# Sample tokens' attention and the merge of attention groups beside head 0's projection, instead of in a stage of their own

## The reference

```
proj = rms_norm(x) @ w_in          # attention q/k/v of 3 groups | DeltaNet q/k/v | z | beta | decay | gates
# for each group g, head h:
s = q_g . k_g * HD_A**-0.5 + bias_g          # keys at distances 0, d, 2d, ..., window
m = max(s); p = exp(s - m); den = sum(p)
o_g = (p / den) @ v_g;   lse_g = m + log(den)
o_a = sum_g softmax_g(lse_g) * o_g           # the merge of the groups
# branch B: gated DeltaNet, 8 heads, chunk by chunk: conv + silu on q/k/v, recurrence, gated norm
mix = sigmoid(gate_a) * (o_a @ w_branch_a) + sigmoid(gate_b) * (o_b @ w_branch_b)
x = x + rms_norm(mix @ w_out);  x = x + rms_norm(ffn(rms_norm(x)))
```

## Time and profile before

| what | value |
|---|---|
| time, median of 3 runs (lowest, highest) | 2573.39 us (2572.24, 2573.95) |
| the profiled execution's own time | 2572.3 us |
| its span, first to last instruction | 2570.5 us |
| TensorE busy (matmul) | 2314.8 us, 90% |
| VectorE, ScalarE, GpSimd busy | 1068.8, 649.0, 30.4 us |
| mean granted TensorE clock | 0.93 |

### The profile page before, as it was taken

One profiled execution on the slowest core, in us unless ns is written; L12 is line 12 of the kernel. 1 busy time (PEld: TensorE's weight loads), 2 busy tenths in 40 slices (PEclk: granted clock), 3 DMA queues, 4 the chain that ended last, 5 costly groups with the idle time before them and its releaser, 6 DMA issues. The chain is left out here.

```text
span 2570.5 us, 35425 instructions
## 1 busy us (share of the span) xinstructions
PE 2314.8 (90%) x13936; PEld 2149.8 (84%) x13936; DVE 1068.8 (42%) x1959; ACT 649.0 (25%) x1428; POOL 30.4 (1%) x28
## 2 busy tenths in 40 slices
PE   5888988559999999999999688796999999979898
PEld 3677877459999999999999588576999999958676
DVE  4123221344776666667666533442222222231233
ACT  4122222103233332323323210442111111131221
POOL 0000000000000000000000000000000000000000
PEclk6999988559999999999999899898999999989999
DMA  4010201411121221212212153623221222050432
GB/s 149 18 64 11 81 11 50 146 29 49 46 70 35 78 58 45 76 28 78 58 45 91 45 168 111 195 84 91 74 71 60 72 67 74 25 173 24 140 110 62
DMA packets 209578, 190.33 MB, mean 74 GB/s; under 512 B 30243, under 2 KB 180804, under 8 KB 209478
## 3 DMA queue, kind: packets, MB, share of 16 engines
q1 hardware_dynamic: 196090, 144.12, 19.1%
q10 hardware_dynamic: 11120, 36.96, 3.7%
q0 software_dynamic: 2304, 8.39, 1.4%
HBM read 138.05 MB, written 51.59 MB: 74 GB/s over the span
## 5 line engine op out<-in xcount | busy, mean ns | idle before, releaser
L270 PE MATMUL bank<-xT_hi,w_lo 128*128 128x344 f32 x1152 | 394.3, 342 | 3.6 <-DVE w_lo L266 3.6
L272 PE MATMUL bank<-xT_hi,w_hi 128*128 128x344 f32 x1152 | 369.4, 321 | 0.0
L271 PE MATMUL bank<-xT_lo,w_hi 128*128 128x344 f32 x1152 | 369.2, 320 | 0.0
L270 PE MATMUL bank<-xT_hi,ffn_lo 128*128 128x344 f32 x1056 | 338.7, 321 | 11.4 <-DVE ffn_lo L266 11.4
L272 PE MATMUL bank<-xT_hi,ffn_hi 128*128 128x344 f32 x1056 | 338.2, 320 | 0.0
L271 PE MATMUL bank<-xT_lo,ffn_hi 128*128 128x344 f32 x1056 | 337.6, 320 | 0.0
L270 PEld LDWEIGHTS bank<-xT_hi,w_lo 128*128 128x128 f32 x1152 | 218.7, 190 | 3.7 <-issue 3.7
L271 PEld LDWEIGHTS bank<-xT_lo,w_hi 128*128 128x128 f32 x1152 | 218.7, 190 | 0.0
L272 PEld LDWEIGHTS bank<-xT_hi,w_hi 128*128 128x128 f32 x1152 | 217.6, 189 | 0.0
L270 PEld LDWEIGHTS bank<-xT_hi,ffn_lo 128*128 128x128 f32 x1056 | 199.5, 189 | 11.5 <-issue 11.5
L272 PEld LDWEIGHTS bank<-xT_hi,ffn_hi 128*128 128x128 f32 x1056 | 199.3, 189 | 0.0
(11 more groups left out here) (364 smaller groups left out, 4106.1 us busy)
## 6 DMA issues: line engine op xcount, KB each, us to landing
w_raw<-in_w_in SPq DMA_DIRECT2D x48, 512.0 KB, 3.9
ffn_raw<-in_w_ffn_in SPq DMA_DIRECT2D x44, 512.0 KB, 5.0
act_scr<-ffn_y ACTq DMA_DIRECT2D x22, 516.0 KB, 2.7
fo_sr<-act_scr SPq DMA_DIRECT2D x16, 704.0 KB, 6.7
fo_wr<-in_w_ffn_out SPq DMA_DIRECT2D x22, 512.0 KB, 5.4
gate_scr<-gate ACTq DMA_DIRECT2D x16, 516.0 KB, 3.3
a_kv_raw<-in_w_in SPq DMA_DIRECT2D x3, 2048.0 KB, 9.2
mix_ta<-gate_scr SPq DMA_DIRECT2D x8, 516.0 KB, 4.9
```

What stands on the lines that cost most here:

```text
L270: nc.tensor.matmul(out, stat_lo, mov_hi, start=start, stop=False)
L271: nc.tensor.matmul(out, stat_hi, mov_lo, start=False, stop=False)
L272: return nc.tensor.matmul(out, stat_hi, mov_hi, start=False, stop=stop)
```

## The change

`sample_attention_block` is gone, and the `clear_semaphores` behind it. Its work stands in `heads_block`, between the steps of head 0's projection. `pipelined` takes a `prologue` for each engine, which gets the `Filler` of head 0 and says between which steps what stands. In detail:

- The queries are no longer spread by TensorE. VectorE writes them to `q_row`, a DMA takes them to `q_scr` in DRAM, and a DMA for each group reads them back for all 128 partitions (`q_all`, 8 KB for each partition). The product with the keys reads both operands from SBUF, 2,048 columns in one instruction.
- Keys and values of the caches are loaded apart (`sa_k`, two buffers; `sa_v`), over tiles that the recurrence uses later. The constants' rows lie in `sa_v` too.
- The own keys and values take a way through DRAM (`kvs_scr`, three more small stores in `attention_block`).
- The merge: only denominators and maxima (`m_stats`, runs of 8 numbers) go to VectorE, which makes the weights; the adding up is done by GpSimd (`merge_rows`), token tile by token tile, five instructions of 256 columns and one load of `m_x` for each of 8 tiles. The result `merged` is turned at the head of `pair_block("mix")`. `os_` keeps the denominators and maxima behind the outputs for that.
- `ub` is cleared behind the prologue, after `merge_over`; TensorE, ScalarE and GpSimd wait for it (`cleared`) before the recurrence.
- GpSimd clears the norm stage's 15 semaphores inside `attention_block`; the single `clear_semaphores` behind `heads_block` has 152 to clear (before: 75 and 100).

```diff
-        def sample_attention_block():
-            with ExitStack() as s, nc.Block() as block:
...
+            def scores(v, g):
+                k = NKEY[g]
+                v.wait_ge(k_ld[g % 2], 16 * (g // 2 + 1))
+                v.wait_ge(q_ld, 16 * g + 16)
+                nc.vector.tensor_tensor(k_c[g % 2][:k], k_c[g % 2][:k], q_all[:k], ALU.mult).then_inc(vec, 1)
+                made(v, "q_used", 2 * g + 1)
+                nc.vector.reduce_sum(sc[:k, g], k_c[g % 2][:k].rearrange("p b (h d) -> p (b h) d", h=HA), AX.X
+                                     ).then_inc(vec, 1)
...
+                for t in range(NT):
+                    pool.wait_ge(x_ld[t % 2], 16 * (t // 2) + 16)
...
+                    nc.gpsimd.tensor_tensor(y, of[0], weight[0], ALU.mult)
+                    nc.gpsimd.tensor_tensor(of[1], of[1], weight[1], ALU.mult)
+                    nc.gpsimd.tensor_tensor(of[2], of[2], weight[2], ALU.mult).then_inc(row, 1)
+                    pool.wait_ge(row, 3 * t + 1)
+                    nc.gpsimd.tensor_tensor(y, y, of[1], ALU.add).then_inc(row, 1)
+                    pool.wait_ge(row, 3 * t + 2)
+                    nc.gpsimd.tensor_tensor(y, y, of[2], ALU.add).then_inc(row, 1)
+                    pool.wait_ge(row, 3 * t + 3)
+                    if t + 2 < NT:
+                        fetch(t + 2)
...
-                    constants_turn(pe)
-                    constants_over(pe)
-                    pipelined(pe, project_pe, recur_pe, lag=0)
+                    def prologue(fill):
+                        sa_turn_q(pe)
+                        constants_turn(pe)
+                        constants_over(pe)
+                        sa_bias(pe)
+                        fill.upto(SC_STEP)
+                        sa_turn_sc(pe)
+                        fill.upto(P_STEP)
+                        sa_turn_p(pe)
+                        fill.upto(PV_STEP)
+                        sa_products(pe)
+                        fill.finish()
+                        pe.wait_ge(cleared, 1)
...
+                    def prologue(fill):
+                        fill.upto(1)
+                        merge_exps(act)
+                        fill.upto(SC_STEP)
+                        sa_exps(act)
+                        fill.finish()
+                        nc.scalar.preload_act_table_set("natural_log_exp_and_others")
+                        act.wait_ge(cleared, 1)
...
-                    nc.vector.memset(ub[:], 0.0).then_inc(cleared, 1)
-                    constants_take(v)
+                    def prologue(fill):
+                        sa_q(v)
+                        constants_take(v)
+                        merge_weights(v)
+                        fill.upto(1)
+                        sa_scores(v, 0)
+                        fill.upto(76)
+                        sa_scores(v, 1)
+                        fill.upto(88)
+                        sa_scores(v, 2)
+                        fill.upto(SC_STEP - 3)
+                        sa_softmax(v)
+                        sa_probs(v)
+                        fill.upto(PV_STEP - 2)
+                        sa_take(v)
+                        fill.finish()
+                        merge_over(v)
+                        nc.vector.memset(ub[:], 0.0).then_inc(cleared, 1)
```

More of the change, by code:

```diff
@@ L502, in attention_block, with _ @@
                 oso = [sem("a_oso") for _ in range(2)]
-                KVO = (2, 5, 9)
+                KVO = (3, 6, 10)
                 done = sums(NT * [KT + 1])
                 SPLIT_Q = 4
+                @block.gpsimd
+                def _(pool):
+                    for x in used:
+                        pool.sem_clear(x)
                 def inc(ins, name):
@@ L1489, in _, with constant_steps @@
                         tiles_of(v, q, stage, split_weights, finish, turn_in)
+        norm_sems = list(live)
         attention_block()
-        sample_attention_block()
-        clear_semaphores()
+        for x in norm_sems:
+            nc.release_semaphore(x)
+            live.remove(x)
         att_stack.close()
-        def constant_steps(s):
-            rows = sb(s, "cs_rows", [CS, 3 * D])
+        def constant_steps(rows):
             ld, tr, ev_ = sem("cs_ld"), sem("cs_tr"), sem("cs_ev")
@@ new lines, in merge_steps, with made, load, exps @@
+        def merge_steps(s, vec, exped):
+            def made(eng, n):
+                eng.wait_ge(vec, VECTOR["merge"] + n)
+            x = [sb(s, f"m_x{j}", [P, NG, HA * HS]) for j in range(2)]
+            stats = sb(s, "m_stats", [P, NG, NT, 2, HA]); top = sb(s, "m_top", [P, NT, HA])
+            f = sb(s, "m_f", [P, NG, NT, HA]); z = sb(s, "m_z", [P, NG, NT, HA])
+            st_ld = sem("m_stats")
+            x_ld = [pool_sem("m_x") for _ in range(2)]
+            row = sem("m_row")
+            def load(sp):
+                for g in range(NG):
+                    sp.dma_start(stats[:, g].rearrange("p t n h -> p t (n h)"),
+                                 att_scr[g].rearrange("(t p) w -> p t w", p=P)[:, :, DEN:]).then_inc(st_ld, 16)
+            def exps(act):
+                made(act, 3)
+                nc.scalar.activation(f[:], f[:], ACT.Exp).then_inc(exped, 1)
+            def weights(v):
+                v.wait_ge(st_ld, 48)
+                mx, den = stats[:, :, :, 1], stats[:, :, :, 0]
+                nc.vector.tensor_tensor(top[:], mx[:, 0], mx[:, 1], ALU.max).then_inc(vec, 1)
+                made(v, 1)
+                nc.vector.tensor_tensor(top[:], top[:], mx[:, 2], ALU.max).then_inc(vec, 1)
+                made(v, 2)
+                for g in range(NG):
+                    last = nc.vector.tensor_tensor(f[:, g], mx[:, g], top[:], ALU.subtract)
+                last.then_inc(vec, 1)
+                v.wait_ge(exped, 1)
+                for g in range(NG):
+                    last = nc.vector.tensor_tensor(z[:, g], f[:, g], den[:, g], ALU.mult)
+                last.then_inc(vec, 1)
+                made(v, 4)
+                nc.vector.tensor_tensor(top[:], z[:, 0], z[:, 1], ALU.add).then_inc(vec, 1)
+                made(v, 5)
+                nc.vector.tensor_tensor(top[:], top[:], z[:, 2], ALU.add).then_inc(vec, 1)
+                made(v, 6)
+                nc.vector.reciprocal(top[:], top[:]).then_inc(vec, 1)
+                made(v, 7)
+                for g in range(NG):
+                    last = nc.vector.tensor_tensor(f[:, g], f[:, g], top[:], ALU.mult)
+                last.then_inc(vec, 1)
+            def rows(pool):
+                def fetch(t):
+                    pool.dma_start(x[t % 2][:], att_scr[:, t * P:(t + 1) * P].rearrange("g p w -> p g w")
+                                   ).then_inc(x_ld[t % 2], 16)
+                for t in range(2):
+                    fetch(t)
+                made(pool, 8)
+                for t in range(NT):
+                    pool.wait_ge(x_ld[t % 2], 16 * (t // 2) + 16)
+                    y = merged[:, t].rearrange("p (h d) -> p h d", h=HA)
+                    of = [x[t % 2][:, g, :DEN].rearrange("p (h d) -> p h d", h=HA) for g in range(NG)]
+                    weight = [f[:, g, t].unsqueeze(2).to_broadcast([P, HA, HD]) for g in range(NG)]
+                    nc.gpsimd.tensor_tensor(y, of[0], weight[0], ALU.mult)
[8 more added lines that the diff above has]
+                        fetch(t + 2)
+            def over(eng):
+                eng.wait_ge(row, 3 * NT)
+            return load, exps, weights, rows, over
@@ L1610, in heads_block, with pipelined @@
             TAIL = SCAN + NT
-            def pipelined(eng, project, recur, lag=1, between=lambda: None):
-                Filler(project(eng, 0, None)).finish()
-                between()
+            def pipelined(eng, project, recur, lag, prologue):
+                prologue(Filler(project(eng, 0, None)))
                 with eng.Fori(0, HB - 1) as i:
@@ L2236, in _, with load @@
                     constants_load(sp)
-                    sp.wait_ge(cleared, 1)
-                    def load(h, prev, recur=False):
+                    def load(h, prev, recur=False, first=None):
                         for m, kind in turn_tiles(h).items():
+                            if first is not None and first != (m < 4):
+                                continue
                             if m == 3 and recur:
@@ L2282, in _ @@
                 def _(pool):
+                    merge_rows(pool)
+                    pool.wait_ge(cleared, 1)
                     for h in range(HB):
```

471 lines of the change are left out of this document (231 added, 240 removed).

## The result

The changed kernel took 2587.58 us (median of 5 runs, 2583.80 to 2592.04) against 2573.39 us before (median of 5 runs, 2568.77 to 2574.92). The ratio is 1.0058, with a 95% interval of 1.0043 to 1.0074: **slower by 0.6%, or 14 us**. I had forecast 2543 us, and 2522 to 2558 as the range.

A forecast was written before the change was run, and what follows sets the result against it. TensorE, busy for 90% of the span, was taken as the bound. Removing 84.0 us, less 13.7 (first product), 37.8 (projection) and 2.2 (ends), saves 30.3: 2543 us forecast, range 2522 to 2558.

The forecast's parts named there:

- Everything below is what comes back: Opens the costs set against the 84.0 us removed: first product, head 0's projection and the ends.
- first product: Head 0's first product: stage begins 84.0 us earlier, product comes 28.7 us into it instead of 15.0, costing 13.7.
- projection of head 0: First product to projection's end: 86.1 us instead of 48.3, +37.8, with the sample work between its steps.
- TensorE's wait for the probabilities: In head 0's projection: TensorE waits 8 us for VectorE's softmax, 3 without GpSimd's disturbance.
- value products with the own ones: In head 0's projection: 24 us, mostly at clock 0.50; at 1.00 they would take 13.
- behind the last head's store: After `heads_block`: 52 more semaphores to clear cost 2.2 us, at most 4.4.
- runs twice as fast: Bound on the first product: `m_stats` loading at twice the assumed rate would save 2.5 us.
- Rival 1: Head 0's projection: clock holds and GpSimd disturbs nobody, ending 21 us sooner, 2522 us; chance 0.12.
- Rival 2: Loads before the first product: short runs slow or backlog delays small loads, 7 us later, 2550 to 2555; chance 0.2.
- Rival 3: Head 0's projection: GpSimd's 256-column steps cost up to 1.89 us, holding VectorE 32 us, 2565 to 2570; chance 0.08.
- Rival 4: Prologue steps simply add to TensorE's path, 2560 us; a stronger form of rivals 2 and 3, no separate chance.
- GpSimd's hold on VectorE: Between the second `w_lo` and softmax: GpSimd steps hold VectorE's two-SBUF-operand steps, 5 us within 0 to 9.

The follow-up runs named there:

- pad_both: Changed kernel plus already-met waits, 133 instructions on TensorE and 30 on VectorE, so the loop over heads begins in blocks as before; 2537.81 us, ratio 0.9863.
- before_shift: Kernel before plus already-met waits, 123 instructions on TensorE and 98 on VectorE, so its loop begins in blocks as in the changed kernel; 2630.80 us, ratio 1.0230.
- late_products: Changed kernel with smaller padding by met waits; probabilities turned at step 138 instead of 126, value products behind step 144 instead of 132; 2532.42 us, ratio 0.9846.
- pad_interleave: On top of pad_both: the value products spread between the last projection steps, in effect 16 ahead of each of six steps; 2542.01 us, ratio 0.9885.
- pad_few_adds: On top of pad_both: four of GpSimd's five merge instructions per token tile cut from 256 to 4 columns; 2536.55 us, ratio 0.9865.
- pad_dve: Changed kernel plus pad_both's 30 instructions of met waits on VectorE alone; 2589.07 us, ratio 1.0062.
- pad_pe: Changed kernel plus pad_both's 133 instructions of met waits on TensorE alone; 2569.65 us, ratio 0.9987.

## Why the prediction was wrong

**The step that failed** is the one that isn't in the sum: "Sum. 84.0 - 13.7 - 37.8 - 2.2". Behind the projection of head 0 I let the loop over heads be as long as before. It took 48.9 us more, since the engines fetched its instructions anew in six of its seven turns. The prediction put that at nothing without a reason: "Everything below is what comes back" looked only at the moved work and at the stages' ends. pad_both and before_shift show the cause from both sides: the place of the loop in the engines' instruction lists decides it. The terms that were in the sum came out: pad_both, with the loop put right, is 5 us below the forecast. The rivals had nothing of the kind either, and the range ended at 2558.

The terms that were in the sum, against the changed kernel's own trace:

| term | forecast | measured |
|---|---|---|
| first product (84.0 less, 13.7 more) | -70.3 | 510.84 - 584.17 = -73.3 |
| projection of head 0, first product to last `z_half` | +37.8 | 87.1 - 48.3 = +38.8 |
| TensorE's wait for the probabilities | 8 | 7.86 |
| value products with the own ones | 24 | 589.3 - 565.2 = 24.1 |
| six turns of the loop | 0 | +48.9 |
| behind the last head's store | +2.2 | 1108.4 - 1106.1 = +2.3 |

With -1.3 for the last head (87.2 instead of 88.6 from mark to mark) these make +15.4 (the third and fourth row lie inside the second); the spans differ by 15.3. The first product was 3 us early because VectorE began at 501.1 instead of 503.3 and was through in 9.7 us instead of 10.5, although the stage itself began at 486.5 and not at 485.1. One bound was wrong in its arithmetic: runs twice as fast would have saved 2 us of 4.1, not 2.5. With the loop put right, pad_both's profiled execution is 35.5 us shorter than that of before, where I had 30.3: 1.5 of the difference stand at the end of the projection (last `z_half` at 598.52), the turns are 0.2 us shorter each, and the 2.2 us behind the last head did not come.

**The rivals.** Rival 1 (the clock holds): no; the granted clock was 1.00 until 568 us, 2 us into the value products, and 0.50 from there to their end, as forecast ("may be up for the first few microseconds and then fall"). The forecast left the cause open. late_products shows that the products bring it down themselves; my belief ahead of pad_interleave, that a dense step between them would restore it, was wrong. Rival 2 (short runs slow): no. The issue of `m_stats` took 6.55 us in the changed kernel, but it began at 491.4, behind the issue of two weight tiles, and in the 2 us from 497 to 499 there went 2,046 packets of under 512 bytes, 1.0 per ns, where I had taken 0.75 and the rival 0.28 (from 491 to 501 there are 3,413 such packets, and `m_stats` is 3,072 runs). The small loads landed 2 us sooner than forecast. Rival 3 (a slow GpSimd step): no; its rows of 256 columns take 0.61 to 0.74 us, and up to 2.67 beside a VectorE instruction. Rival 4 (the change hides nothing): no.

**GpSimd's hold on VectorE, 5 us by forecast:** from the second tile's `w_lo` to the softmax VectorE took 27.7 us (526.5 to 554.2) for 23 of instructions by my count. Taken at the shortest that each kind took in the changed kernel, pad_both or pad_few_adds, the rows of this stretch make 22.0 us, and the other 5.7 stand in rows that overlap one of GpSimd's. The largest is a `w_lo` beside four instructions of a token tile; here it is in the changed kernel with the last of GpSimd's that it overlaps, and then in pad_few_adds:

```profile
544.61 2.87 DVE L271 TENSOR_TENSOR w_lo<-w_raw,w_hi 128x1024 fp32r<-128x1024 f32 x1
...
546.47 1.61 POOL L1588 TENSOR_TENSOR merged<-merged,m_x 128x256 f32<-128x256 f32 x1
```

```profile
550.06 1.21 DVE L271 TENSOR_TENSOR w_lo<-w_raw,w_hi 128x1024 fp32r<-128x1024 f32 x1
```

In pad_few_adds the same stretch takes 23.4 us without the wait for the queries, in pad_both 25.6. That fits the 5 us of the sum, in kind too. It is a reading of rows, though: pad_few_adds prices only 2.3 us, on top of pad_both, and no run took GpSimd's work out of the changed kernel itself.

The Trainium skill, "Runtime: NRT & Kernel Launch", Instruction fetch mechanics, holds the mechanism: a taken branch whose target isn't in the current window of 2 pages forces a fetch before execution goes on. It gives TensorE 128 KiB and most other engines 32 KiB, in blocks of 16 KiB. The traces agree on the stall, and on TensorE's packets of 16 KB. They differ on the rest: VectorE's packets are of 8 KB, and TensorE's body of 1,609 instructions, over 100 KB at 64 bytes each, is jumped back over without a packet in the kernel before, so it holds more than 2 blocks. The same section says that the cost of crossing a block is mostly hidden. The loop's first turn agrees: it was fetched in both kernels (7 and 6 large packets from the last `z_half` on) and took 104.9 and 104.8 us. The jump back is what is not hidden.

## What to carry to other kernels

Before an edit ahead of a long hardware loop, look at the instruction queues' rows: no packets in a turn means that the body fits where it stands, not that it will fit where an edit ahead of it shifts it, on each engine apart. How near the border is, the packets don't say; the body's length against what is held does. An idle time with releaser "issue" at the loop's head, on several engines at once and every turn, is the sign; a few instructions that do nothing, put where the engine idles, settle it, and must be put on every engine that fetches. When a change slows a kernel, compare the length of a loop's turn early on, in the code that wasn't touched too.

## What the runs showed of the hardware that I had not expected

- A turn's fetching costs TensorE 7.9 us and VectorE 5.2, both together 8.1, of a turn of 106.4, for bodies of 1,609 and 269 instructions (pad_dve, pad_pe, the changed kernel).
- A wait that is already met is not free: 133 instructions of two such waits each took TensorE 12.6 us (498.7 to 511.3 in pad_both), 98 took VectorE 10.0 (before_shift), some 0.1 us for an instruction.
- Products with 128x128 weights and two columns brought the granted clock from 1.00 to 0.50 while TensorE was busy for all of the time (late_products, 570 to 580 us). They did so too with three dense matmuls of 344 columns behind every 16 of them (pad_interleave, 0.50 from 570 to 595 us).
